# Last layer norm of a hybrid decoder step: five of 17 tiles closed by ScalarE and GpSimd instead of VectorE

## The reference

```
h = layer_norm(ALPHA * x + mix, ln1_g, ln1_b)
f = hier_moe(h)
y = layer_norm(ALPHA * h + f, ln2_g, ln2_b)

layer_norm(x, g, b):  (x - mean(x)) * rsqrt(var(x) + 1e-5) * g + b      # over the 1024 columns
```

## Time and profile before

| | |
|---|---|
| median of 3 runs | 1383.74 us (1380.58 to 1384.69) |
| the profiled execution | 1386.9 us |
| its span, first to last instruction | 1385.0 us |
| VectorE busy | 734.4 us (53%) |
| ScalarE busy | 539.4 us (39%) |
| GpSimd busy | 472.4 us (34%) |
| TensorE busy | 1276.4 us (92%) |
| the last addition into the rows in HBM issued | 1324.2 us |
| loads of the last layer norm | issued from 1330.4 us on |
| its first and last VectorE operation | 1338.30, and 1381.38 + 1.27 us |

### The profile page before, as it was taken

How to read it: one execution, slowest core, us unless ns; L and a number is a source line. 1 busy time by engine, 2 the same in 40 slices (tenths; PEclk the granted TensorE clock), 3 DMA queues, 4 the chain that set the end, 5 groups by cost and what they waited for, 6 DMA issues and landing times.

```text
span 1385.0 us, 21099 instructions
## 1 busy us (share of the span) xinstructions
PE 1276.4 (92%) x5477; PEld 607.3 (44%) x5478; DVE 734.4 (53%) x2079; ACT 539.4 (39%) x881; POOL 472.4 (34%) x640
## 2 busy tenths in 40 slices
PE   8999999989999988799999999999999999999910
PEld 3434444657666655355545555433333333333300
DVE  2423333463655555568888997344444444444338
ACT  0000101333445343323333331266665666656544
POOL 5112210000000000355555563344666566666312
PEclk9999999999999999999999999999999999999965
DMA  6354533222112165256655552269989999999776
GB/s 260 106 198 157 178 119 111 77 92 77 65 50 77 61 208 165 89 210 225 220 199 178 166 153 77 72 183 318 318 261 369 355 283 316 332 365 368 208 245 277
DMA packets 89957, 269.70 MB, mean 195 GB/s; under 512 B 14496, under 2 KB 40672, under 8 KB 76742
## 3 DMA queue, kind: packets, MB, share of 16 engines
q1 hardware_dynamic: 72903, 223.90, 45.2%
q0 software_dynamic: 14144, 41.26, 12.4%
q10 hardware_dynamic: 2823, 3.54, 0.8%
HBM read 209.66 MB, written 63.25 MB: 197 GB/s over the span
## 4 chain that ended last, share of the span: by engine, by line
PE 49%; issue 29%; DVE 9%; DMA 5%; DVEq 4%; ACT 1%; POOL 1%; SPq 1%; POOLq 1%; ACTq 0%
PE P L1032 13%; PE bank_S L1054 10%; PE M L1032 6%; PE bank_S L701 4%; PE P L701 3%; PE bank_T L701 2%; PE P L904 2%; PE bank_S L874 2%; DMA work<-conv_rows 2%; DVEq L1577 2%; PE M L701 2%; DVE route L1582 1%; PE M L1040 1%; DMA big<-sum_rows 1%; DVE work L1539 1%
## 5 line engine op out<-in xcount | busy, mean ns | idle before, releaser
L1272 ACT ACTIVATE big<-big 128x2048 f32 x78 | 148.9, 1910 | 155.4 <-issue 113.3
L1032 PE MATMUL P<-big,work 128*64 x416 | 188.0, 595 | 1.8 <-DVE work L1759 1.6
L1033 PE MATMUL P<-big,work 128*64 128x512 f32 x416 | 188.0, 595 | 0.0
L740 PE MATMUL P<-big,work 128*128 128x256 f32 (+1 forms) x512 | 173.6, 496 | 0.0
L1928 POOL DMA_INDIRECT work<-h_rows,piece_idx x152 | 145.8, 959 | 72.1 <-issue 51.4
L1054 PE MATMUL bank_S<-big,work 128*64 x312 | 140.4, 593 | 2.5 <-issue 1.5
L1056 PE MATMUL bank_S<-big,work 128*64 128x512 f32 x312 | 140.4, 593 | 0.0
L1865 POOL TENSOR_SCALAR work<-work 128x1 f32<-128x1 f32 (+1 forms) x17 | 3.8, 221 | 376.7 <-DVE work L1465 376.7
L740 PEld LDWEIGHTS P<-big,work 128*128 128x128 f32 x512 | 97.3, 194 | 70.4 <-issue 63.6
L874 PE MATMUL P<-big,work 128*128 128x512 f32 x256 | 113.8, 597 | 3.5 <-DVE work L1496 3.5
L874 PE MATMUL bank_S<-big,work 128*128 128x512 f32 x256 | 115.5, 605 | 0.0
(11 more groups left out here) (310 smaller groups left out, 2274.6 us busy)
## 6 DMA issues: line engine op xcount, KB each, us to landing
big<-in_w SPq DMA_DIRECT2D x96, 1024.0 KB
work<-in_xt_prompt SPq DMA_DIRECT2D x32, 512.0 KB, 3.5
big<-sum_rows SPq DMA_DIRECT2D x16, 520.0 KB, 8.9
big<-in_toe SPq DMA_DIRECT2D x16, 512.0 KB, 3.3
work<-in_x_prompt SPq DMA_DIRECT2D x16, 512.0 KB, 4.0
h_rows<-work SPq DMA_DIRECT2D x16, 512.0 KB
sum_rows<-work SPq DMA_DIRECT2D x16, 512.0 KB
out_y_prompt<-big SPq DMA_DIRECT2D x16, 512.0 KB
```

The lines of the kernel that those rows point to most:

```text
L740: last = mm(dst[0:n, 0:c1 - c0], lhs[:, k, :], w_qkv[:, k, c0:c1], start=(k == 0), stop=(k == KD - 1))
L1032: mm(lower, xgT[j][:, k, 0:U], both[:, k], start=(k == 0), stop=(k == KD - 1))
L1033: last = mm(upper, xgT[j][:, k, U:P], w_up[:, k], start=(k == 0), stop=(k == KD - 1))
L1272: fn(w_up.rearrange("p k m f -> p m k f")[:, :, ks, :], src, ACT.Copy).then_inc(s[f"wu{part}_ok"], 1)
```

## The change

Tiles 2, 5, 8, 11 and 14 (`SHARED`) are centred by VectorE as before. Their closing is split: ScalarE multiplies the tile by its rstd (`scaled`), after VectorE's centring (new semaphore `c_ct`) and after the power (`c_rs`); its place in ScalarE's program is behind the statistics of tile t + 2. GpSimd then adds `ln_b`, after ScalarE (`c_sc`); its place in GpSimd's program is behind the power of the pair that holds tile t + 3 (tile 16 for tile 14). VectorE skips `finished(t)` for them. SP waits for GpSimd's semaphore `c_yb` ahead of their stores, and stores in the order `STORED`: 0, 1, 3, 4, 2, 6, 7, 5, 9, 10, 8, 12, 13, 11, 15, 14, 16. The other twelve tiles are closed by VectorE.

```diff
+        SHARED = (2, 5, 8, 11, 14)
+        STORED = [t for q in range(0, NT - 1, 3) for t in (q, q + 1, q - 1)[0 if q else 0:3 if q else 2]] + [NT - 1, NT - 2, NT]
...
@@ SP
-            for t in range(NT + 1):
+            for t in STORED:
                 n = rows_of(t)
-                after(sp, s["c_yv"], t)
+                if t in SHARED:
+                    after(sp, s["c_yb"], SHARED.index(t))
+                else:
+                    after(sp, s["c_yv"], t - sum(q < t for q in SHARED))
...
@@ ScalarE
+            def scaled(t):
+                zz = out_t[:, t, 0:D]
+                act.wait_ge(s["c_rs"], 1 + part_of(t, RSTD))
+                after(act, s["c_ct"], SHARED.index(t))
+                fn(zz, zz, ACT.Copy, scale=c_rs[:, t:t + 1]).then_inc(s["c_sc"], 1)
...
+                if t - 2 in SHARED:
+                    scaled(t - 2)
...
@@ VectorE
-                stt(zz, zz, c_mv[0:n, t, 0:1], ln_g[0:n, :], ALU.subtract, ALU.mult)
+                last = stt(zz, zz, c_mv[0:n, t, 0:1], ln_g[0:n, :], ALU.subtract, ALU.mult)
+                if t in SHARED:
+                    last.then_inc(s["c_ct"], 1)
...
-                if step >= LAG:
+                if step >= LAG and step - LAG not in SHARED:
                     finished(step - LAG)
...
@@ GpSimd
+            g.wait_ge(s["ln2_in"], 32)
             for lo, hi in RSTD:
...
+                for q, t in enumerate(SHARED):
+                    if lo <= min(t + 3, NT) < hi:
+                        after(g, s["c_sc"], q)
+                        gtt(out_t[:, t, 0:D], out_t[:, t, 0:D], ln_b, ALU.add).then_inc(s["c_yb"], 1)
```

More of the change, by code:

```diff
@@ L167 @@
 wu0_ok wu1_ok wd_ok pe_mid xg_in0 xg_in1 xg_in2 w0_ld w1_ld w2_ld y_out0 y_out1 pe_up pe_gT pe_dn xgT_ev a_sig g_ok gT_ev y_ev0 y_ev1
-ln2_in c_in0 c_in1 c_in2 c_in3 c_in4 c_in5 c_va c_rs c_yv c_out
+ln2_in c_in0 c_in1 c_in2 c_in3 c_in4 c_in5 c_va c_rs c_yv c_ct c_sc c_yb c_out
 """.split()
@@ L351, in layer @@
         LAG = 3
+        SHARED = (2, 5, 8, 11, 14)
+        STORED = [t for q in range(0, NT - 1, 3) for t in (q, q + 1, q - 1)[0 if q else 0:3 if q else 2]] + [NT - 1, NT - 2, NT]
+        assert sorted(STORED) == list(range(NT + 1))
         def part_of(t, parts):
```

## The result

The changed kernel takes 1388.14 us in the median of 22 runs (1382.44 to 1392.87), the kernel before 1382.01 us in 22 runs beside them (1378.74 to 1386.34). The medians are 6.1 us apart. The ratio of the two kernels is 1.004, 95% interval 1.0028 to 1.0052: by it the changed kernel is slower by 5.5 us, between 3.9 and 7.2. The forecast was +6.05 us.

A forecast was written before the change was run, and what follows sets the result against it. VectorE was taken to set the end of the last layer norm. Closings removed (-6.8), additions holding VectorE (+10.5) and crowded stores (+2.35) sum to +6.05 us on 1383.74: 1389.8 us, range 1385.3 to 1392.2.

The forecast's parts named there:

- What goes: Last layer norm, VectorE: five closings (tiles 2, 5, 8, 11, 14) leave its path, -6.8 us.
- ScalarE and the added waits: Last stage: ScalarE's five scalings hide behind a slowed VectorE, 0 us; GpSimd's queued powers cost 0, at most 1 us.
- the forecast's 1.6 us: Last stage: without the slowing of VectorE, ScalarE would set the pace, 0.4 us a period, 1.6 us in all.
- The additions: Last stage: each of five GpSimd additions holds VectorE's two-SBUF-input operations 2.1 us, +10.5 us.
- The middle part together: From the end of VectorE's fourth centring (tile 3) to its last operation's end: VectorE ends 3.7 us later.
- The stores: End of span: four large stores, delayed by the new order, leave within VectorE's last 2.75 us, +2.35 us.
- The sum: Whole kernel: -6.8 + 10.5 + 2.35 = +6.05 us, giving 1389.8 us from a median of 1383.74.
- Rival 1: Last stage: GpSimd's additions read between VectorE's accesses without exclusion; -2.85 us, 1380.9 us; chance 0.10.
- rival 2: End of span: the store queue hides its crowding, only the exclusion is paid; +3.7 us, 1387.4 us; chance 0.15.
- rival 3: Last stage: additions take 2.8 us beside VectorE; +2.2 us on the sum, 1392.0 us; chance 0.13.
- Rival 4: Last stage: tile 14's addition slips behind VectorE's end; 1388.9 us; chance 0.62 together with the forecast.

The follow-up runs named there:

- e1_psum_weights: Changed kernel with VectorE's second tensors (ln_g, ln_b) copied to PSUM by VectorE; 1379.65 us against 1380.77 for the kernel before, ratio 0.9983.
- e4_tiny_add: Changed kernel with GpSimd adding the bias to 2 columns of each shared tile, not 1024, all waits kept; 1377.54 us against 1380.77 before, ratio 0.997.
- e3_store_order: Changed kernel with stores in the order in which its tiles are ready; 1387.09 us against 1380.77 for the kernel before, ratio 1.003.
- e2_before_psum: Kernel before, all tiles closed by VectorE, with VectorE's second tensors copied to PSUM by VectorE; ratio 1.0008 to the kernel before.
- e8_scalar_copies: Changed kernel with VectorE's second tensors copied to PSUM by ScalarE and stores in order 0 to 16; 1377.94 us against 1381.98 before, ratio 0.997.

## Why the prediction was right

**What goes, -6.8 us.** Right: e1_psum_weights shows 38.7 - 31.8 = 6.9 us in the middle part when neither the additions nor ScalarE's pace take it back.

**ScalarE and the added waits, 0 beside the stall.** Right: with the additions in place VectorE waited once more for ScalarE, 0.32 us before centring 6, and this wait ran into the time of an addition that would have held VectorE anyway. Without the stall the forecast's 1.6 us appear, 1.4 in e4_tiny_add. The scalings take 1135 ns, by the row of the first layer norm 1149.

**The additions, +10.5 us.** Right, and this term carried the forecast. VectorE's five held operations stood still for 1.7, 2.1, 2.1, 2.1 and 2.45 us, 10.4 in all. The 1.7 of the first and the 0.4 by which centring 6 came late for ScalarE are together 2.1. The place of the last was missed: the prediction had tile 14's addition begin when only centring 16 and closings 13, 15 and 16 were left; it held closing 12, ahead of these, and for 2.45 us, because it stood from its own issue on, 0.32 us ahead of the addition, and through it. This is the one addition whose price was off, by 0.35 us.

**The middle part together.** Forecast +3.7, measured 42.7 - 38.7 = +4.0 in both the changed kernel and e3_store_order; the last addition's 0.35 us is the difference.

**The stores, +2.35 us.** Right: 4.7 - 2.35 = 2.35 us, and taken back to 2.4 us by the order of stores alone. The rate over the 5.5 us was 387 GB/s, the not quite full first and last slice with it. The 358 GB/s of the Trainium skill's table (SBUF — State Buffer, A bandwidth-pool intuition that's wrong), which the prediction weighed beside it, is below what this run measured, and the measurement decides.

**The sum.** The profiled stages differ by 5.5 us, because in the changed kernel's execution the rows of tiles 2 and 3 happened to land earlier: ScalarE took up tile 2 after 7.5 us without a wait, and after 8.4 us with one of 1.02 before, so that centring 3 ends at 12.7 and not 13.5. The seven experiments, whose loads are the same, have 8.1 to 9.1 us there, so this is scatter. With it set aside the edit costs 4.0 + 2.35 = 6.35, against the forecast's 6.05 and the 5.5 (3.9 to 7.2) of the timed runs. The 1389.8 us itself stood on a start of 1383.74, the median of three runs; from the 1382.01 of 22 runs the same sum gives 1388.1, and 1388.14 was measured. That it comes so close is partly luck, since the runs tell no more than 3.9 to 7.2 us. Rival 1 (no exclusion) is what e1_psum_weights had to build; rival 2 (stores hidden) is refuted by e3_store_order and the 4.7 us; rival 3 (additions of 2.8 us beside VectorE) was half seen: their records do show 2753 ns, but 0.4 of that is waiting, and VectorE is held for 2.1 in the mean. Rival 4 (tile 14's addition slips behind VectorE's end) did not happen: that addition came 8.7 us before VectorE's end.

**One reading was wrong**, without a part in the sum. I took the 14.9 us before VectorE's first centring for a wait on ScalarE, as the row says. In e1_psum_weights and e2_before_psum the first operation there is a copy that waits only for weights whose load was issued at 866 us, 470 us before, and it starts 14.87 us after VectorE's previous instruction; the centring starts 14.95 us after it in every other kernel, whenever the statistics came. So this time passes in VectorE's own program, between the loop over the blocks and the next stage. What it does there no run here shows. In these 15 us of the kernel before three packets of the instruction queue move, as against four in the 123 us ahead of them, but the trace does not say for which engine. In such a row the releaser is the last event that could have been waited for, and not always what held the engine. A slip of the pen beside it: 0.56 + 0.13 in the chances is 0.69 and not 0.68.

## What to carry to other kernels

Before work is moved from VectorE to GpSimd to run beside it, count the SBUF tensors that VectorE's instructions read there: with two, a GpSimd instruction that reads SBUF runs instead of them and not beside them, and here 2.35 us on GpSimd took the place of 1.28 us on VectorE. Putting the second tensor into PSUM (here row weights, copied once for 1.2 us each by VectorE or 1.0 by ScalarE) took the exclusion away, and with it the same split shortened the stage from 54.6 to 51.4 us (e1_psum_weights, and e8_scalar_copies with another order of stores). A stall of this kind stands in the mean length of the instructions and not in the list of waits, so both have to be read. When a rearranged stage stores through one in-order queue, order the stores by when the tiles are ready, and look at how many large ones are left behind the last operation.

## What the runs showed of the hardware that was not expected

- A VectorE instruction that is issued before a GpSimd addition can be held through that addition all the same. Closing 12 was issued at 1371.95, 0.32 us before the addition of 1372.27, while the power of 1370.75 was ending; it stood still through that addition too, 2.45 us and not 2.1. e3_store_order shows the same to a hundredth (closing issued at 1374.54, addition at 1374.86, 3.73 and 2.33 us). It is not so always: in the changed kernel centring 6 was let in between the addition of 1342.71, which ended at 1345.59, and the power issued at 1345.62, and it was the power that waited (1.62 us). What decides who is next no run here shows.
- The GpSimd powers of 128x2 take 0.69 to 0.73 us each when VectorE has one tensor in PSUM (698 ns in the mean in e1_psum_weights), and up to 1.55 where both are in SBUF, though a power reads only two columns.
- VectorE needs 14.95 us from its last instruction in the loop over the blocks to the first one behind it, the same in all seven kernels that begin the stage with a centring. ScalarE's first instruction behind its loop, the copy in e8_scalar_copies, comes 7.87 us after the last one.
